# The experts' four stationary buffers moved 64 bytes off the 512-byte grid, in an encoder kernel on one Trainium2 core

## The chip, the cores and the metric

The kernel runs on one core of one Trainium2 chip. The metric is the device time of one execution in microseconds (us). Before the change it is 1674.84 us, the median of 3 runs (1674.06 to 1678.73).

## What is computed

Two sequences (`x_prompt` and `x_sample`, 512 tokens of 1024 channels each) go through one encoder layer with shared weights: RMSNorm, neighbourhood attention with 16 heads, a residual, RMSNorm, an expert-choice mixture of 16 SwiGLU experts, a residual and a last RMSNorm. All arrays are float32. The part that the change touches is the mixture of experts. Each expert takes the 64 tokens of each sequence that it scores highest:

```
aff = jax.nn.softmax(jnp.einsum('nd,de->ne', xf, router_w).astype(jnp.float32), axis=-1)
gate, idx = lax.top_k(aff.T, cap)
xs = xf[idx]
hid = jax.nn.silu(jnp.einsum('ecd,edf->ecf', xs, w_gate)) * jnp.einsum('ecd,edf->ecf', xs, w_up)
out = jnp.einsum('ecf,efd->ecd', hid, w_down) * gate[..., None].astype(xs.dtype)
y = jnp.zeros_like(xf).at[idx.reshape(-1)].add(out.reshape(-1, D).astype(xf.dtype))
```

Here `cap` is 64, the experts' width is 2048, and both sequences together give each expert 128 rows.

## The kernel before

The kernel is written by hand, engine by engine: SyncE issues the loads of weights, GpSimd gathers and scatters rows, ScalarE, VectorE and TensorE compute, and semaphores order them. Nothing is scheduled by a tool; each engine runs its instructions in the order of the code.

**Products.** A float32 product is made of three matmuls of type float32r. Every operand is split into a high part (a cast to float32r) and a rest (the value minus its high part). `products` (L1118) issues for each pair of operands high x high, high x rest and rest x high into the same PSUM bank. All its matmuls stand on line L1123. In a trace row `ps<-w_high,xt_high 128*128 128x512` the first name is the moving operand (its 512 columns stream through the array), the second the stationary one (128 x 128 values that are loaded into the array first). The load of the stationary operand is an instruction of its own in the trace, LDWEIGHTS, on a row of the engine named PEld.

**Ahead of the experts.** For each of the two sequences the normed input stands transposed in `ut_high` and `ut_rest`. Four groups of four heads follow: `project_t` makes queries and keys (the weights are stationary, 512 columns of `ut` move), `project_v` makes the values (blocks of `ut` are stationary, 256 columns of the weights move), `score`, `turn_probabilities`, `values` and `project_out` do the rest. In `values` (L1228) the stationary operand is a slice of `v` or `v_off` of one head, 64 columns or 256 bytes. The router follows, with the choice of the tokens on VectorE.

**The experts.** A loop over the 16 experts runs on every engine. The 128 gathered rows (`xg`) are transposed on TensorE (`rows_t`, L1379), ScalarE writes their high part into `xt_high` (`rows_high`, L693) and VectorE the rest into `xt_rest` (`rows_rest`, L1053). `gate_up` makes one half of the hidden width at a time: 8 pairs of weight tiles, 96 matmuls, stationary `xt_high` and `xt_rest`. The product of both branches, `hid`, is transposed (`hidden_t`, L1409) and split into `ht_high` (L697) and `ht_rest` (L1057). `down` multiplies by the other weights: 4 pairs, 48 matmuls, stationary `ht_high` and `ht_rest`. So an expert has 2 x 96 + 2 x 48 = 288 matmuls, each with 512 moving columns. Every tile of weights (1 MB, 128 x 2048 values) is loaded into `raw`, `raw_more` or `early`, cast by ScalarE into one of four slots of `w_high` (L713) and split by VectorE into `w_rest` (L779). In the last expert the second `down` takes `xt_high` and `xt_rest` as its stationary buffers (written on L756 and L1085).

**Where the buffers lie.** `sb` takes a buffer where the one before it ends. `sb_line` rounds its start up to a multiple of `LINE` = 512 bytes (in each of the 128 partitions). All large buffers are made by `sb_line`, so a moving block of 512 columns (2048 bytes) and a stationary one of 128 columns (512 bytes) both begin on this grid. In the program as built `xt_high` starts at byte 22016 (43 x 512), `xt_rest`, `ht_high` and `ht_rest` behind it, 4096 bytes each, and `raw_more` at 38400. `w_high` starts at 87552 and `w_rest` at 120320. `ut_high` starts at 22016 as well; it and the experts' buffers share the space, one after the other in time. `ident`, the moving operand of the transposes, starts at 16512, 128 bytes past a grid line.

Of the kernel before, what the change touches and what calls it, by code (L numbers as in the profile page):

```python
# [18 lines left out]
F32R = mybir.dt.float32r  # L19
# [5 lines left out]
P = 128  # L25
D = 1024
# [28 lines left out]
HALF = F // 2  # L55
BANK = 512
LINE = 512
FRONT_Q = TRUNKS * GROUPS
GU_PAIRS = 8
D_PAIRS = 4  # L60
# [50 lines left out]
def encoder_kernel(nc, x, g_mix, g_ffn_col, g_ffn, g_fin, w_qkv, bias, w_o, router_w, w_gate, w_up, w_down, identity, y):  # L111
# [5 lines left out]
    with ExitStack() as ctx:  # L117
        def sb(name, shape, dt=F32):
            return ctx.enter_context(nc.sbuf_tensor(name, shape, dt))
# [30 lines left out]
        def sb_line(name, shape, dt=F32):  # L150
            return ctx.enter_context(nc.sbuf_tensor(name, shape, dt, align_bytes=LINE))

        with ExitStack() as front:
            ut_high = front.enter_context(nc.sbuf_tensor("ut_high", [P, KC * T], F32R, align_bytes=LINE))
            ut_rest = front.enter_context(nc.sbuf_tensor("ut_rest", [P, KC * T], F32R, align_bytes=LINE))
        xt_high, xt_rest = sb_line("xt_high", [P, D], F32R), sb_line("xt_rest", [P, D], F32R)
        ht_high, ht_rest = sb_line("ht_high", [P, D], F32R), sb_line("ht_rest", [P, D], F32R)
        raw_more = sb_line("raw_more", [P, 2, PAIR])
        raw = sb_line("raw", [P, SLOTS, PAIR])
        w_high = sb_line("w_high", [P, SLOTS, PAIR], F32R)  # L160
# [6 lines left out]
        with ExitStack() as attention:  # L167
            v_off = attention.enter_context(nc.sbuf_tensor("v_off", [P, TILES - 1, GC], F32, align_bytes=LINE))
            bias_sb = attention.enter_context(nc.sbuf_tensor("bias_sb", [P, 2, 3, WIN], F32, align_bytes=LINE))
            ot_high = attention.enter_context(nc.sbuf_tensor("ot_high", [P, 2, T], F32R, align_bytes=LINE))  # L170
            ot_rest = attention.enter_context(nc.sbuf_tensor("ot_rest", [P, 2, T], F32R, align_bytes=LINE))
# [102 lines left out]
        def body_q(e, i):  # L274

            return FRONT_Q + GU_PAIRS // SLOTS + (2 * (GU_PAIRS + D_PAIRS) // SLOTS) * e + i // SLOTS

        def body_turn(e, i):

            return GU_PAIRS // RAW_SLOTS + (2 * (GU_PAIRS + D_PAIRS) // RAW_SLOTS) * e + i // RAW_SLOTS  # L280

        def pairs_before(e):

            return SLOTS * (body_q(e, 0) - FRONT_Q)

# [22 lines left out]
        def _(sp):  # L308

            def load(q, j, src):  # L310
                if not (isinstance(q, int) and q == 0):

                    sp.wait_ge(rest_done, SLOTS * (q - 1) + j + 1)
                sp.dma_start(raw[:, j, :].rearrange("p (k n) -> p k n", k=src.shape[1]), src).then_inc(raw_in[j], 16)  # L314

            def gate_up_rows(e, h, jj):
                rows_ = (w_gate, w_up)[jj % 2][bass.ds(e * D + (jj // 2) * 2 * P, 2 * P), h * HALF:(h + 1) * HALF]
                return rows_.rearrange("(k p) n -> p k n", p=P)
# [11 lines left out]
            def load_first(i):  # L330

                if i < SLOTS:
                    return load(FRONT_Q, i, gate_up_rows(0, 0, i))
                if i < SLOTS + 2:
# [176 lines left out]
        def _(act):  # L511
# [193 lines left out]
            def highs(e, lo, hi):  # L705

                for i in range(lo, hi):
                    q, before = (FRONT_Q + i // SLOTS, 0) if e is None else (body_q(e, i), body_turn(e, i))

                    act.wait_ge(pair_used, SLOTS * (q - FRONT_Q - 1) + i % SLOTS + 1)  # L710

                    act.wait_ge(raw_in[i % RAW_SLOTS], 16 * ((FRONT_Q if i % RAW_SLOTS < SLOTS else 0) + before + 1))
                    nc.scalar.copy(w_high[:, i % SLOTS, :], raws[i % RAW_SLOTS]).then_inc(high_done, 1)  # L713
# [765 lines left out]
```

## Time and profile before

| | before |
|---|---|
| median of 3 runs | 1674.84 us (1674.06 to 1678.73) |
| the profiled execution | 1675.15 us |
| its span, first to last instruction | 1673.3 us |
| mean granted TensorE clock | 0.979 |
| TensorE busy | 1590.2 us (95%) |
| VectorE busy | 1279.0 us (76%) |
| ScalarE busy | 1052.2 us (63%) |
| first matmul of the experts | 553.67 us into the span |

The profiled execution lies 1.85 us above its span; that part is outside the first and the last instruction. Busy time is the time in which an engine had at least one instruction under way; matmuls overlap each other, so the duration of one is longer than the distance to the next. The granted clock is given as a share of 2.4 GHz.

### The profile page before, as it was taken

To read this page: it belongs to the slowest core of one execution; us is meant where nothing else is said; L and a number is where in the kernel's file an instruction comes from. 1 tells how busy PE (TensorE), PEld (TensorE's weight loads), DVE (VectorE), ACT (ScalarE), POOL (GpSimd) and SP (SyncE) were. 2 spreads that over 40 slices of the span, in tenths; PEclk is the share of its full clock that TensorE was granted. 3 is DMA by queue.
4 is the path that set the end of the run, shared out by engine and by line. 5 is a ranking of instruction groups with operands and counts; after the bars stand their busy time and mean duration, and the time that the engine had idled before them with its cause. 6 is when DMAs were issued, how large, how long until landed. Compare 5 with 4: busy or idle time off the path is not lost.

```text
span 1673.3 us, 22439 instructions
## 1 busy us (share of the span) xinstructions
PE 1590.2 (95%) x8198; PEld 1322.8 (79%) x8198; DVE 1279.0 (76%) x1259; ACT 1052.2 (63%) x940; POOL 119.1 (7%) x65
## 2 busy tenths in 40 slices
PE   5999999999994799999999999999999999999993
PEld 4888787888783688888888888888888888888882
DVE  5554575554566588888888888888888888888886
ACT  4443355443343477777777777777777777777774
POOL 0000002000002001011010110100101101011011
PEclk9999999999996899999999999999999999999997
DMA  9333243533253699999999999999999999999993
GB/s 355 123 104 112 79 155 144 199 105 107 85 186 139 223 342 367 393 398 376 392 380 387 397 370 386 390 384 397 365 392 397 376 393 380 387 392 375 392 393 142
DMA packets 150326, 496.14 MB, mean 296 GB/s; under 512 B 9488, under 2 KB 34192, under 8 KB 150288
## 3 DMA queue, kind: packets, MB, share of 16 engines
q1 hardware_dynamic: 138848, 454.20, 71.8%
q0 software_dynamic: 10160, 38.28, 7.0%
q10 hardware_dynamic: 1280, 3.15, 0.7%
q8 instruction: 25, 0.41, 0.1%
q14 instruction: 13, 0.11, 0.0%
HBM read 471.47 MB, written 20.97 MB: 294 GB/s over the span
## 4 chain that ended last, share of the span: by engine, by line
PE 89%; DVE 4%; DMA 2%; ACT 2%; SPq 1%; issue 1%; ACTq 0%; DVEq 0%; POOL 0%; POOLq 0%
PE ps L1123 80%; PE ps L1197 2%; PE ps L1228 2%; PE ps L1409 2%; PE ps L1206 2%; PE ps L1328 1%; PE ps L1379 1%; DMA arena<-h_rows 1%; DVE w_rest L779 1%; DMA h_rows<-xh,rows 1%; SPq L314 1%; PE ps L1317 1%; DVE arena L812 0%; DMA rw<-router_w 0%; SPq L380 0%
## 5 line engine op out<-in xcount | busy, mean ns | idle before, releaser
L779 DVE TENSOR_TENSOR w_rest<-raw,w_high 128x2048 fp32r<-128x2048 f32 x224 | 510.3, 2290 | 98.4 <-ACT w_high L713 65.3
L713 ACT CAST w_high<-raw 128x2048 fp32r<-128x2048 f32 x188 | 360.2, 1916 | 138.2 <-PE ps L1123 138.2
L1123 PE MATMUL ps<-w_high,xt_high 128*128 128x512 f32 x1040 | 324.4, 393 | 3.9 <-DVE xt_rest L1053 2.4
L1123 PE MATMUL ps<-w_rest,xt_high 128*128 128x512 f32 x1040 | 321.2, 390 | 0.0
L1123 PE MATMUL ps<-w_high,xt_rest 128*128 128x512 f32 x1040 | 320.9, 390 | 0.0
L779 DVE TENSOR_TENSOR w_rest<-raw_more,w_high 128x2048 fp32r<-128x2048 f32 x96 | 218.6, 2290 | 48.6 <-ACT w_high L713 48.6
L779 DVE TENSOR_TENSOR w_rest<-early,w_high 128x2048 fp32r<-128x2048 f32 x96 | 218.5, 2289 | 23.0 <-ACT w_high L713 21.5
L1123 PEld LDWEIGHTS ps<-w_rest,xt_high 128*128 128x128 f32 x1040 | 195.8, 188 | 41.1
L1123 PEld LDWEIGHTS ps<-w_high,xt_rest 128*128 128x128 f32 x1040 | 195.8, 188 | 41.0
L1123 PEld LDWEIGHTS ps<-w_high,xt_high 128*128 128x128 f32 x1040 | 193.2, 188 | 43.3 <-DVE xt_rest L1053 2.8
L713 ACT CAST w_high<-raw_more 128x2048 fp32r<-128x2048 f32 x96 | 183.9, 1916 | 69.0 <-PE ps L1123 69.0
L713 ACT CAST w_high<-early 128x2048 fp32r<-128x2048 f32 x96 | 183.9, 1916 | 61.4 <-PE ps L1123 61.4
L1123 PE MATMUL ps<-w_high,ht_high 128*128 128x512 f32 x496 | 154.2, 392 | 0.0
L1123 PE MATMUL ps<-w_high,ht_rest 128*128 128x512 f32 x496 | 152.8, 389 | 0.0
L1123 PE MATMUL ps<-w_rest,ht_high 128*128 128x512 f32 x496 | 152.8, 389 | 0.0
L528 ACT ACTIVATE arena<-arena,nmx 128x256 f32<-128x256 f32 x128 | 63.6, 498 | 89.7 <-DVE nmx L827 89.7
L1123 PEld LDWEIGHTS ps<-w_rest,ht_high 128*128 128x128 f32 x496 | 93.1, 188 | 19.5
L1123 PEld LDWEIGHTS ps<-w_high,ht_rest 128*128 128x128 f32 x496 | 93.1, 188 | 19.4
L487 POOL DMA_INDIRECT h_rows<-xh,rows x15 | 37.5, 2502 | 973.2 <-ACT xh L703 973.2
L1123 PE MATMUL ps<-ut_high,w_high 128*128 128x512 f32 x256 | 103.2, 403 | 3.4 <-DVE w_rest L779 3.4
L1123 PEld LDWEIGHTS ps<-w_high,ht_high 128*128 128x128 f32 x496 | 91.9, 188 | 18.1
L1123 PE MATMUL ps<-ut_rest,w_high 128*128 128x512 f32 x256 | 100.4, 392 | 0.0
(152 smaller groups left out, 1937.9 us busy)
## 6 DMA issues: line engine op xcount, KB each, us to landing
raw<-w_gate SPq DMA_DIRECT2D x64, 1024.0 KB, 7.4
raw<-w_up SPq DMA_DIRECT2D x64, 1024.0 KB, 8.1
raw<-w_down SPq DMA_DIRECT2D x64, 1024.0 KB, 7.4
raw_more<-w_gate SPq DMA_DIRECT2D x32, 1024.0 KB, 7.9
raw_more<-w_up SPq DMA_DIRECT2D x32, 1024.0 KB, 8.8
early<-w_gate SPq DMA_DIRECT2D x32, 1024.0 KB, 8.4
early<-w_up SPq DMA_DIRECT2D x32, 1024.0 KB, 8.5
raw_more<-w_down SPq DMA_DIRECT2D x32, 1024.0 KB, 7.6
```

The source lines that it names most:

```text
L314: sp.dma_start(raw[:, j, :].rearrange("p (k n) -> p k n", k=src.shape[1]), src).then_inc(raw_in[j], 16)
L487: pool.indirect_dma_start(h_dram, bass.IndirectOffsetOnAxis(ap=rows[:, e:e + 1], axis=0), ys, None, compute_op=ALU.add).then_inc(scattered ...
L528: nc.scalar.activation(scores[hh % 2][:, i, :], scores[hh % 2][:, i, :], ACT.Exp, bias=nmx[:, hh % 2, i:i + 1], accum_out=psum_row[:, hh % ...
L713: nc.scalar.copy(w_high[:, i % SLOTS, :], raws[i % RAW_SLOTS]).then_inc(high_done, 1)
L779: nc.vector.tensor_tensor(w_rest[:, j, :], raws[j if r is None else r], w_high[:, j, :].bitcast(F32), ALU.subtract).then_inc(rest_done, 1)
L1123: done = nc.tensor.matmul(out, lhs, rhs, start=start and part == 0, stop=stop and part == 2)
L1197: last = nc.tensor.matmul(ps[:, 6 * BANK + at:6 * BANK + at + WIN], qt[on, p, tile * P:(tile + 1) * P], kt[on, p, lo:lo + WIN], start=True ...
L1206: last = nc.tensor.transpose(ps[:, at:at + P], scores[hh % 2][:, i, c * P:(c + 1) * P], ident[:, :])
L1228: last = nc.tensor.matmul(bank(4)[a * HD:(a + 1) * HD, tile * P:(tile + 1) * P], vals, pt[:, at:at + P], start=c == 0, stop=c == 1)
L1317: last = nc.tensor.transpose(bank(ROUTER_BANKS[i % 2], 2)[:, kc * P:(kc + 1) * P], xh[:, i, kc * P:(kc + 1) * P], ident[:, :])
L1328: last = nc.tensor.matmul(bank(4)[:, i * E:(i + 1) * E], rt[i % 2][:, kc * P:(kc + 1) * P], rw[:, kc, :], start=kc == 0, stop=kc == KC - 1)
L1409: last = nc.tensor.transpose(bank(6, 2)[:, c * P:(c + 1) * P], hid[:, c * P:(c + 1) * P], ident[:, :])
```

## The change

The four buffers `xt_high`, `xt_rest`, `ht_high` and `ht_rest` are no longer made by `sb_line` but by a new helper that rounds a start up to 64 bytes only, behind a buffer `shift` of 64 bytes that nothing reads or writes. In the program as built each of the four starts 64 bytes lower than before: `xt_high` at 21952, which is 448 bytes past a grid line or 64 bytes short of the next. `shift` lies at 21888. Every other buffer keeps its address, and on every engine the instructions, their order and their waits are the same. A stationary block of 512 bytes, which began on a grid line and ended on the next, now begins 64 bytes ahead of a line and crosses it.

```diff
@@ -55,6 +55,7 @@
 HALF = F // 2
 BANK = 512
 LINE = 512
+SHIFT = 64
 FRONT_Q = TRUNKS * GROUPS
 GU_PAIRS = 8
 D_PAIRS = 4
@@ -153,8 +154,11 @@
         with ExitStack() as front:
             ut_high = front.enter_context(nc.sbuf_tensor("ut_high", [P, KC * T], F32R, align_bytes=LINE))
             ut_rest = front.enter_context(nc.sbuf_tensor("ut_rest", [P, KC * T], F32R, align_bytes=LINE))
-        xt_high, xt_rest = sb_line("xt_high", [P, D], F32R), sb_line("xt_rest", [P, D], F32R)
-        ht_high, ht_rest = sb_line("ht_high", [P, D], F32R), sb_line("ht_rest", [P, D], F32R)
+        def sb_shift(name):
+            return ctx.enter_context(nc.sbuf_tensor(name, [P, D], F32R, align_bytes=SHIFT))
+
+        sb("shift", [P, SHIFT // 4])
+        xt_high, xt_rest, ht_high, ht_rest = (sb_shift(n) for n in ("xt_high", "xt_rest", "ht_high", "ht_rest"))
         raw_more = sb_line("raw_more", [P, 2, PAIR])
```

## Rows read from the trace of the kernel before

**Rows 1.** The page: busy us of each engine, share, instructions.
```profile
PE 1590.2 (95%) x8198; PEld 1322.8 (79%) x8198; DVE 1279.0 (76%) x1259; ACT 1052.2 (63%) x940; POOL 119.1 (7%) x65
```

**Rows 2.** The page: the chain that ended last, by engine and by line.
```profile
PE 89%; DVE 4%; DMA 2%; ACT 2%; SPq 1%; issue 1%; ACTq 0%; DVEq 0%; POOL 0%; POOLq 0%
PE ps L1123 80%; PE ps L1197 2%; PE ps L1228 2%; PE ps L1409 2%; PE ps L1206 2%; PE ps L1328 1%; PE ps L1379 1%; DMA arena<-h_rows 1%; DVE w_rest L779 1%; DMA h_rows<-xh,rows 1%; SPq L314 1%; PE ps L1317 1%; DVE arena L812 0%; DMA rw<-router_w 0%; SPq L380 0%
```

**Rows 3.** The chain in order of time, one expert: start us, us, what.
```profile
671.80 0.87 PE ps L1379 x8
672.67 10.90 PE ps L1123 x48
683.57 0.87 PE ps L1409 x8
684.45 32.66 PE ps L1123 x144
717.11 0.87 PE ps L1409 x8
717.98 21.78 PE ps L1123 x96
739.76 0.87 PE ps L1379 x8
```

**Rows 4.** Busy time by stretch, two experts: PE, PEld, DVE, ACT, POOL, clock, DMA.
```profile
672.67:740.63 67.96, 67.96 (x314) 56.54 (x313) 59.95 (x30) 51.36 (x31) 5.28 (x2) 1.00 1.02 391
740.63:808.59 67.96, 67.96 (x314) 56.54 (x313) 59.95 (x30) 51.39 (x31) 5.27 (x2) 1.00 1.01 380
```

**Rows 5.** Groups of TensorE by line: busy us, mean ns, idle before, releasers.
```profile
L1123 PE MATMUL ps<-w_high,xt_high 128*128 128x512 f32 x1040 | 324.4, 393 | 3.9 <-DVE xt_rest L1053 2.4 <-DVE xt_rest L1085 1.0 <-DVE w_rest L779 0.6
...
L1123 PE MATMUL ps<-w_high,ht_high 128*128 128x512 f32 x496 | 154.2, 392 | 0.0
```

**Rows 6.** Timeline of TensorE in `project_v`: start us, us, instruction.
```profile
349.07 0.28 PE L1123 MATMUL ps<-w_high,ut_rest 128*128 128x256 f32 x1
...
350.51 0.28 PE L1123 MATMUL ps<-w_high,ut_rest 128*128 128x256 f32 x1
```

**Rows 7.** Line L1228, the loads: duration ns least/median/most, first and last start us.
```profile
L1228 PEld LDWEIGHTS ps<-arena,v x256: 132/137/137, 69.4 to 495.6; 128*64 128x64 f32 x128
...
L1228 PEld LDWEIGHTS ps<-arena,v_off x256: 132/137/137, 69.7 to 495.2; 128*64 128x64 f32 x128
```

**Rows 8.** Instructions on the tiles `xt_high` and `ht_high`, same columns.
```profile
L1123 PEld LDWEIGHTS ps<-w_high,xt_high x1040: 186/188/333, 553.7 to 1646.8; 128*128 128x128 f32 x174
...
L693 ACT CAST xt_high<-ps x16: 999/1007/1012, 551.3 to 1558.0; 128x1024 fp32r<-128x1024 f32 x16
L1053 DVE TENSOR_TENSOR xt_rest<-ps,xt_high x16: 1214/1216/1224, 552.4 to 1560.6; 128x1024 fp32r<-128x1024 f32 x16
...
L697 ACT CAST ht_high<-ps x31: 999/1011/1012, 589.4 to 1608.8; 128x1024 fp32r<-128x1024 f32 x31
L1057 DVE TENSOR_TENSOR ht_rest<-ps,ht_high x31: 1216/1218/1220, 591.7 to 1611.1; 128x1024 fp32r<-128x1024 f32 x31
```

**Rows 9.** The chain in order of time, where the experts begin.
```profile
552.39 1.24 DVE xt_rest L1053
553.67 21.66 PE ps L1123 x84
```

**Rows 10.** The page: GB/s that the DMA engines moved, 40 equal slices.
```profile
GB/s 355 123 104 112 79 155 144 199 105 107 85 186 139 223 342 367 393 398 376 392 380 387 397 370 386 390 384 397 365 392 397 376 393 380 387 392 375 392 393 142
```

**Rows 11.** The chain in order of time: two pieces of the output projections.
```profile
426.20 5.67 PE ps L1123 x24
...
492.18 2.78 PE ps L1123 x12
```

## The prediction

> **What bounds the kernel now.** I read four views, from coarse to fine. The page's busy times come first: TensorE is busy for 95% of the span, VectorE for 76%, ScalarE for 63% [rows 1]. A busy share does not say who sets the end, so the chain of work that ended last comes next: 89% of it is TensorE, and 80% of the span is one line, L1123, the matmuls of `products` [rows 2]. The third view is the same chain in order of time, through one expert [rows 3]. The reader should see that nothing but TensorE stands in it: 48 + 144 + 96 = 288 matmuls in 10.90 + 32.66 + 21.78 = 65.34 us, three times eight transposes of 0.87 us, and again from the start. The fourth view, busy time by stretch, says the same of whole experts: of 67.96 us TensorE is busy for 67.96, VectorE for 59.95, ScalarE for about 51.4, at a granted clock of 1.00, which is the 2.4 GHz level [rows 4]. So in the experts the pace is set by TensorE's own distance from one matmul to the next, 65.34 us / 288 = 226.9 ns. No wait stands there for another engine to shorten or lengthen.
>
> **How many matmuls the change can reach.** The four moved buffers are the stationary operand of 3 x 1040 matmuls (`xt_high`, `xt_rest`) and 3 x 496 (`ht_high`, `ht_rest`), 4608 in all [rows 5]. Their cost now is 4608 x 226.9 ns = 1045.6 us, 62% of the span. One nanosecond per matmul is thus 4.6 us, and what a measurement of this kernel can tell from no change, about 0.3% or 5.0 us, is 1.1 ns per matmul. This is the number to watch: a very small effect of the address would show.
>
> **What the 226.9 ns are made of.** The matmuls of `project_v` have 256 moving columns in place of 512. In the timeline 12 of them follow each other from 349.07 to 350.51 us, 120.0 ns apart [rows 6]. The difference of 106.9 ns for 256 columns is 2.4 columns per ns. So 512 columns stream for 213.8 ns, by the plain 2.4 GHz for 213.3, and each matmul carries a part of about 13.3 ns that does not grow with the columns. (By 2 x 120.0 - 226.9 it is 13.1, by 226.9 - 213.3 it is 13.6; the starts are given to 0.01 us.) That fixed part is the only thing in the experts' pace that an address of the stationary operand could take away. It is the same size here, with stationary blocks of `ut_high` and `ut_rest`, and in the experts. Both of these pairs start on the 512-byte grid, so this alone cannot say whether the grid causes it.
>
> **The load of the stationary operand.** It runs beside the matmul before it. Where nothing longer covers it, its pace is seen: the eight transposes L1379 or L1409 have 128 moving columns only (53 ns at the rate above) and still take 0.87 us / 8 = 108.9 ns each [rows 3]. That is the load's own pace for 128 columns. Beside 512 moving columns it has 226.9 - 108.9 = 118 ns of cover. Each shifted block of 512 bytes starts 64 bytes below a grid line, so it touches two lines of the grid where it touched one. As an estimate take a cost of one more 64-byte piece on eight: 108.9 / 8 = 13.6 ns, hidden in the 118. With the cover gone it would be 4608 x 13.6 ns = 63 us; it would take a load more than twice as long for the cover to go. I cost it at nothing.
>
> Does an offset lengthen a load at all? The trace has a natural trial. In `values` (L1228) the stationary operand is a head's 64 columns, 256 bytes, so that every other head begins 256 bytes off the 512-byte grid. The 256 loads from `v` last 132 to 137 ns with a median of 137, and those from `v_off` the same [rows 7]. Half of each are off the grid, and no second duration appears. Such a block does not cross a grid line, so it excludes a cost of the start, not of the crossing. The transposes give the other half of the trial, for a moving operand off the grid: `ident` starts 128 bytes past a grid line and the pace is still only 2 ns above the 107 ns that 128 columns would take at half the streaming rate [rows 3].
>
> **Do the two reads meet?** The stationary block of 512 bytes is read while 2048 bytes of moving columns are read. By the paces above, one goes at about 512 / 107 = 4.8 bytes per ns and the other at 9.6. With different speeds, two readers that start on the same place of a repeating grid part at once and meet again elsewhere; a start moved by 64 bytes shifts the meetings by some 13 ns and does not remove them. That is a second reason to expect nothing, even if a collision costs something.
>
> The Trainium skill, in "SBUF — State Buffer", section "Who interferes with whom", gives TensorE two independent read ports, one for the moving operand and one for the load, and says that it never waits on another reader. By that rule the stationary operand's place changes nothing and the sum is 1675. No run here has yet shown both of its halves; the constant pace beside a busy DMA and VectorE [rows 3, 4] agrees with it.
>
> **The writes into the buffers.** ScalarE writes `xt_high` in 1.01 us and VectorE `xt_rest` in 1.22 us, 17 times each (16 of them in the row), and `ht_high` and `ht_rest` 31 times each in 1.01 and 1.22 us [rows 8]. If all became an eighth longer, VectorE would gain 48 x 0.152 = 7.3 us of work and ScalarE 6.1 us. Inside an expert that is hidden: VectorE has 67.96 - 59.95 = 8.0 us free in each of them [rows 4]. It is exposed only at the first expert and at the last one's second half, where TensorE waits for `xt_rest`, 2.4 and 1.0 us [rows 5]: 2 x (0.126 + 0.152) = 0.6 us. I take zero, with 0.6 as the upper end.
>
> **Everything else.** The change adds no instruction, no semaphore wait and no DMA, and the order on every engine is the same. `ut_high`, `ut_rest`, `raw_more` and all behind them keep their addresses, since the 64 bytes of `shift` and the move both lie in what was padding. The stages ahead of the experts' matmuls, up to 553.67 us [rows 9], should not change.
>
> **The sum.** Matmuls 4608 x 0, loads 0 (covered), writes 0 (0 to 0.6): 1675.15 us for the profiled execution, which stands 0.3 us above the median of the runs, 1674.84. I forecast 1674.8.
>
> **Rivals.**
>
> No relation or meetings that only move, so no change. For it: two different read speeds, the load with 118 ns of cover, a pace that holds through an expert to 0.1 ns while VectorE, ScalarE and DMA vary. Against it: nothing here pairs an off-grid stationary block with a stream long enough to be the bound. Time 1671 to 1679. **Chance 0.64.**
>
> Faster: the fixed 13.3 ns are the price of both reads starting on the same place of the grid, and the shift removes it. For it: in every group where it can be read, both operands are on the grid. Against it: it is equally large beside 512 and 256 moving columns. Removed whole it would be 4608 x 13.3 = 61 us, or 1614; but then an expert takes 64.1 us, and the weights must come in that time. An expert moves (391 + 380) / 2 GB/s x 67.96 us = 26.2 MB now [rows 4], and the fastest slice of the span shows 398 GB/s [rows 10], at which 26.2 MB take 65.8 us. So DMA becomes the bound after 2.1 us per expert, 16 x 2.1 = 34 us: 1641. A removal in part gives anything between. **Chance 0.15.**
>
> The Trainium skill, "TensorE: Matmul & The Clock Gate", section "Wait — 56ns, not 53.3ns?", gives a warm matmul of 512 columns a start-to-start of 215.7 ns. By that figure 11.2 of the 226.9 ns here are surplus, an estimate of 52 us for the experts. The row here stands above the page, and the page does not say what the surplus is.
>
> Slower: what now runs without a meeting begins to have one. The two reads start within a few ns of each other, on the same grid, and may be in step by luck; shifted, each load crosses a line in its first 64 bytes while the stream begins. The place is each of the 4608 starts. The price has no row of its own. The nearest is the same form of matmul where it runs slower for another reason: 12 in 2.78 us, 231.7 ns, or 24 in 5.67 us, 236.3 ns, both in output projections [rows 11]. That is +4.8 to +9.4 ns, 22 to 43 us: 1697 to 1718. I take the first, nearer to no cost. It decides from 1.1 ns on. For it: the same absence of an off-grid row. Against it: the loads of L1228 show no second duration. **Chance 0.21.**
>
> **The numbers.** The predicted time is that of the likeliest case, 1674.8, whose own range is 1671 to 1679. To leave out no more than 2 in 10 I reach to the near end of the slower rival, 1698, and down to 1668, a gain of 1.5 ns per matmul; the gain of tens of microseconds is left out. Faster by over 0.3% 0.15, within 0.3% 0.64, slower by over 0.3% 0.21.
>
> **What would show it.** Right: in the changed kernel an expert still has 10.90, 32.66 and 21.78 us in the chain, loads from `xt_high` have a median of 188 ns [rows 8], and the start of the experts stays at about 554 us. Wrong in the cover of the load: loads over 188 ns and a pace above 226.9. Wrong in the meeting of reads: the pace changes with loads unchanged. If only the writes matter, L1053 and L1057 differ from 1.22 us and the pace does not. The prediction fails if the pace moves by more than 1.1 ns per matmul either way. A change only in the first 554 us would mean that something other than the buffers' place acts.

## The result and the profile after

The changed kernel takes 1686.03 us (median of 4 runs, 1684.25 to 1688.71), the kernel before 1675.12 us beside it. The ratio is 1.0057 with a 95% interval of 1.0043 to 1.0071: slower, by about 9 to 11 us. On the page of the changed kernel one busy time grew by more than 2 us: TensorE is at 1600.1 us where it was 1590.2 [rows 1]. Its loads (PEld) are at 1324.2 for 1322.8; VectorE and ScalarE moved by 0.1 and 0.6 us.

```profile
PE 1600.1 (95%) x8198; PEld 1324.2 (79%) x8198; DVE 1278.9 (76%) x1259; ACT 1052.8 (63%) x940; POOL 119.2 (7%) x65
```

The chain in order of time through one expert shows where (start us, us, what). All lines are four higher than before, so L1127 is `products`.

```profile
672.82 0.87 PE ps L1383 x8
673.69 10.99 PE ps L1127 x48
684.68 0.88 PE ps L1413 x8
685.55 32.96 PE ps L1127 x144
718.51 0.87 PE ps L1413 x8
719.38 21.97 PE ps L1127 x96
741.36 0.87 PE ps L1383 x8
```

These answer to [rows 3]. The transposes take what they took, 0.87 us. The 288 matmuls take 10.99 + 32.96 + 21.97 = 65.92 us where they took 65.34: 228.9 ns each for 226.9. The same stands in the busy time by stretch, two experts:

```profile
673.69:742.23 68.54, 68.54 (x314) 56.58 (x313) 59.95 (x30) 51.40 (x31) 5.27 (x2) 1.00 1.01 385
742.23:810.77 68.54, 68.54 (x313) 56.58 (x313) 59.95 (x30) 51.41 (x31) 5.28 (x2) 1.00 1.01 380
```

An expert takes 68.54 us for 67.96 [rows 4], with VectorE, ScalarE and the granted clock as they were. 16 x 0.58 = 9.3 us accounts for the growth of the span, 1682.4 us for 1673.3. The chain where the experts begin is no later than before:

```profile
551.41 1.24 DVE xt_rest L1057
552.69 21.33 PE ps L1127 x84
```

And the instructions on the tile `xt_high` (duration ns least/median/most) show what did not change, against [rows 8]:

```profile
L1127 PEld LDWEIGHTS ps<-w_high,xt_high x1040: 186/188/338, 552.7 to 1655.9; 128*128 128x128 f32 x174
...
L697 ACT CAST xt_high<-ps x16: 1001/1005/1012, 550.4 to 1566.6; 128x1024 fp32r<-128x1024 f32 x16
L1057 DVE TENSOR_TENSOR xt_rest<-ps,xt_high x16: 1214/1215/1224, 551.4 to 1569.2; 128x1024 fp32r<-128x1024 f32 x16
```

The load still lasts 188 ns, the writes 1.01 and 1.22 us. So it is neither a longer load that came out of its cover nor the writes: the distance from one matmul to the next grew by 2.0 ns while everything on either side of it kept its size. That is the sign that the prediction had named for a failure in the meeting of the reads: the pace changes with the loads unchanged.

The 2.0 ns are a mean. The trace keeps each start to 1 ns, finer than the views print. In the experts of the kernel before (from 600 to 1600 us, leaving out the first dozen matmuls behind each group of transposes) every start is 226 or 227 ns after the one before it. In the changed kernel three distances take turns, 232, 226 and 229 ns on average, with high and rest blocks alike. So the price is not the same at every matmul; every third one pays none.

### The profile page after: what moved, and what is told of

It reads as the page before. It is cut to its first block, busy times and chain, and to the rows that moved or that the text cites. A ratio compares the mean times of both kernels' runs of the same rounds, so it can differ in the third digit from the quotient of the medians.

```text
span 1682.4 us, 22439 instructions
## 1 busy us (share of the span) xinstructions
PE 1600.1 (95%) x8198; PEld 1324.2 (79%) x8198; DVE 1278.9 (76%) x1259; ACT 1052.8 (63%) x940; POOL 119.2 (7%) x65
## 4 chain that ended last, share of the span: by engine, by line
PE 90%; DVE 4%; DMA 2%; ACT 1%; SPq 1%; issue 1%; ACTq 0%; DVEq 0%; POOL 0%; POOLq 0%
PE ps L1127 80%; PE ps L1201 2%; PE ps L1232 2%; PE ps L1210 2%; PE ps L1413 2%; PE ps L1332 1%; PE ps L1383 1%; DMA arena<-h_rows 1%; DMA h_rows<-xh,rows 1%; SPq L318 1%; DVE w_rest L783 1%; PE ps L1321 0%; DVE arena L816 0%; DMA rw<-router_w 0%; SPq L384 0%
## 5 line engine op out<-in xcount | busy, mean ns | idle before, releaser
L1127 PE MATMUL ps<-w_high,xt_high 128*128 128x512 f32 x1040 | 326.9, 396 | 3.8 <-DVE xt_rest L1057 2.4
L1127 PE MATMUL ps<-w_rest,xt_high 128*128 128x512 f32 x1040 | 324.9, 394 | 0.0
L1127 PE MATMUL ps<-w_high,xt_rest 128*128 128x512 f32 x1040 | 322.2, 391 | 0.0
L1127 PEld LDWEIGHTS ps<-w_high,xt_rest 128*128 128x128 f32 x1040 | 195.8, 188 | 44.7
L1127 PEld LDWEIGHTS ps<-w_rest,xt_high 128*128 128x128 f32 x1040 | 196.3, 189 | 42.7
L1127 PEld LDWEIGHTS ps<-w_high,xt_high 128*128 128x128 f32 x1040 | 193.8, 189 | 43.9 <-DVE xt_rest L1057 2.8
L1127 PE MATMUL ps<-w_high,ht_high 128*128 128x512 f32 x496 | 155.0, 394 | 0.0
L1127 PE MATMUL ps<-w_rest,ht_high 128*128 128x512 f32 x496 | 154.5, 393 | 0.0
L1127 PE MATMUL ps<-w_high,ht_rest 128*128 128x512 f32 x496 | 153.3, 390 | 0.0
L1127 PEld LDWEIGHTS ps<-w_high,ht_rest 128*128 128x128 f32 x496 | 93.1, 188 | 21.3
L1127 PEld LDWEIGHTS ps<-w_rest,ht_high 128*128 128x128 f32 x496 | 93.2, 188 | 20.1
L1127 PEld LDWEIGHTS ps<-w_high,ht_high 128*128 128x128 f32 x496 | 92.0, 188 | 18.4
L1127 PE MATMUL ps<-ut_high,w_high 128*128 128x512 f32 x256 | 103.0, 402 | 2.8 <-DVE w_rest L783 2.8
L1127 PE MATMUL ps<-ut_high,w_rest 128*128 128x512 f32 x256 | 100.5, 393 | 0.0
```

Source lines behind the costliest of these rows:

```text
L1127: done = nc.tensor.matmul(out, lhs, rhs, start=start and part == 0, stop=stop and part == 2)
```

## The experiments

Two theories were put against each other first. **R, relative**: the price hangs on the distance in bytes between the start of the stationary block and that of the moving one; in the trace the load of one runs beside the matmul that streams the other. **C, crossing**: a load that crosses a grid line costs, wherever the moving block lies. "Distance" below is the start of the stationary block less that of the moving one; all blocks start a multiple of 512 bytes from the start of their buffer. In every kernel the instructions and their order are those of before. Where a shifted buffer ends past the line on which the next one began, all buffers behind it that `sb_line` makes start one whole line of 512 bytes later, which leaves their distances as they were in steps of 256. "Pace" is the length of a piece of the chain over its count of matmuls.

**1. Everything 64 bytes below the grid.** The padding is put ahead of `ut_high`, and the alignment lowered to 64 bytes. So the distance is 0 again in `products`, while each of its loads and moving blocks crosses a line.

```diff
-LINE = 512
+LINE = 64
...
+        sb("shift", [P, 16])
+
         def sb_line(name, shape, dt=F32):
```

> All line-aligned buffers, the moving ones too, lie 64 bytes below the 512-byte grid; the distance between a stationary and a moving block is that of the kernel before. Theory R (relative: the price hangs on the distance between the start of the loaded block and that of the moving one): an expert back at 67.96 us, 226.9 ns per matmul, about 1675 us. Theory C (crossing: each load of a block that crosses a grid line costs, wherever the moving one lies): the experts stay at 228.9 ns per matmul, and the projections ahead of them get slower too, about 1686 to 1690 us.

Measured: 1678.98 us beside 1676.64, ratio 1.0009 (95% interval 0.9998 to 1.0019), which is no difference. The chain gives the experts' pace of before to the last digit:

```profile
689.04 32.66 PE ps L1125 x144
722.57 21.78 PE ps L1125 x96
745.23 10.90 PE ps L1125 x48
```

Theory C is out: the loads cross the grid's lines and cost nothing.

**2. The moving buffers 64 bytes past the grid, the stationary ones on it.**

```diff
-        w_high = sb_line("w_high", [P, SLOTS, PAIR], F32R)
-        w_rest = sb_line("w_rest", [P, SLOTS, PAIR], F32R)
+        sb("shift", [P, 16])
+        w_high, w_rest = (ctx.enter_context(nc.sbuf_tensor(n, [P, SLOTS, PAIR], F32R, align_bytes=64))
+                          for n in ("w_high", "w_rest"))
```

> The stationary buffers are on the grid as before, but w_high and w_rest start 64 bytes past it; in the experts the relative distance is that of the changed kernel. Theory R: 228.9 ns per matmul in the experts, about 1686 us, and the projections, where either the stationary or the moving block is w_high or w_rest, slower too. Theory C: loads in the experts do not cross, so 226.9 ns and about 1675 us, unless a moving block that crosses costs as well.

Measured: 1688.19 us beside 1676.64, ratio 1.0067 (1.005 to 1.0084). The experts' pieces of the chain are those of the changed kernel within 0.02 us, although no stationary buffer was moved:

```profile
689.43 32.97 PE ps L1124 x144
...
723.27 21.99 PE ps L1124 x96
...
746.14 10.99 PE ps L1124 x48
```

So R holds: what counts is the distance, here again -64 bytes. This kernel says two things more. In `project_t` the roles are turned (`w_high` is stationary, `ut_high` moves, distance +64), and there the price is larger. Two pieces of 24 matmuls in the chain, the first behind `score` (L1198, which is L1197 in the kernel before), the second behind the eight transposes on L1207 (L1206 before):

```profile
326.07 5.79 PE ps L1124 x24
...
333.91 5.61 PE ps L1124 x24
```

The same two kinds of piece in the same stretch of the kernel before:

```profile
323.49 5.67 PE ps L1123 x24
...
331.20 5.47 PE ps L1123 x24
```

Like against like, 24 matmuls take 0.12 and 0.14 us more, 5.0 and 5.8 ns each; a piece this short holds the first few matmuls too, which come at uneven distances in either kernel. In `project_v` (distance -64, 256 moving columns) the matmuls came *closer* together. The timeline, the first and the last row of a run of them:

```profile
350.13 0.28 PE L1124 MATMUL ps<-w_rest,ut_high 128*128 128x256 f32 x1
...
354.84 0.28 PE L1124 MATMUL ps<-w_high,ut_rest 128*128 128x256 f32 x1
```

The second start is 40 matmuls after the first, 4.71 us / 40 = 117.8 ns, where [rows 6] gave 120.0. With all buffers 64 bytes lower (experiment 1) the pieces of 48 of `project_v` take 5.94 and 5.95 us as before, so this too goes by the distance. The fixed 13.3 ns of the prediction are not a constant of the engine.

**3 and 4. Other distances: 128 and 256 bytes.** In the first the four buffers start at byte 21888 (no padding, alignment 64), in the second 256 bytes past a line.

```diff
-        xt_high, xt_rest = sb_line("xt_high", [P, D], F32R), sb_line("xt_rest", [P, D], F32R)
-        ht_high, ht_rest = sb_line("ht_high", [P, D], F32R), sb_line("ht_rest", [P, D], F32R)
+        sb("shift", [P, 384 // 4])
+        xt_high, xt_rest, ht_high, ht_rest = (ctx.enter_context(nc.sbuf_tensor(n, [P, D], F32R, align_bytes=32))
+                                              for n in ("xt_high", "xt_rest", "ht_high", "ht_rest"))
```

> The four stationary buffers 128 bytes below the grid in place of 64. Theory C: a crossing is a crossing, 228.9 ns per matmul, 1686 us. Theory R: a price that varies with the distance, another pace than 228.9 ns; with a grain of 128 bytes it is 226.9 ns and 1675 us.

> The four stationary buffers 256 bytes off the grid, half a line. Theory C: 228.9 ns per matmul, 1686 us. Theory R with a grain of 128 or 256 bytes: 226.9 ns and 1675 us; with a price that grows with the distance: slower than the changed kernel, over 1686 us.

Measured: 128 bytes 1701.94 us, ratio 1.0144 (1.0127 to 1.0161); 256 bytes 1676.67 us, ratio 1.0 (0.9989 to 1.001). The chain has, for the first and then for the second:

```profile
687.57 33.46 PE ps L1123 x144
```

```profile
685.98 32.66 PE ps L1124 x144
```

That is 232.4 ns per matmul at 128 bytes and 226.8 at 256. At half a line of the grid nothing is lost, though the loads cross a 512-byte line as well. A price that goes on growing with the distance is out, and so is a grain of 128 bytes; what is left is R with a repeat of 256 bytes.

**5 to 7. 32 bytes on either side, and 64 on the other side.** Same edit with paddings of 96, 160 and 192 bytes.

> The four stationary buffers 32 bytes below the grid, half the distance of the change. Theory L (the price grows with the distance up to 128 bytes: 0, 2.1, 5.5 ns at 0, 64, 128): about 227.5 to 228 ns per matmul, 1679 to 1681 us. [...]

> The four stationary buffers 32 bytes past a grid line. Theory L, symmetric: as 32 bytes below. Theory A (the sign matters, as the q and k projections of the kernel with the moved w_high suggest, 64 bytes past at 231 to 236 ns): another pace than 32 bytes below, 228 to 231 ns, 1681 to 1695 us.

> The four stationary buffers 64 bytes past a grid line in place of 64 below. Theory L, symmetric in the distance: 228.9 ns, 1686 us. Theory A: 233 ns per matmul, as the projections with 64 bytes past show, so 28 us more than before, about 1705 us. A start on any other 64-byte place being one and the same cost (crossing) is already out by the run at 256 bytes.

Measured: 32 bytes below 1707.51 us and 32 past 1707.48 us (one run each, beside 1676.32), 64 past 1703.94 us, ratio 1.0163 (1.0146 to 1.0181). The 144 matmuls of the chain:

```profile
692.14 33.59 PE ps L1124 x144
```

```profile
691.77 33.60 PE ps L1124 x144
```

```profile
690.37 33.59 PE ps L1124 x144
```

All three are 233.3 ns. The first theory L, a price that grows with the distance, fell here: 32 bytes cost three times what 64 below do. A price in steps of 64 bytes is out as well, since 32 below has neither the pace of 0 nor that of 64 below. Theory A held for 64 past (233 ns expected and measured), but its number for 32 past, 228 to 231 ns, was too low, and its claim that 32 past differs from 32 below was wrong.

**8. One part of the change alone: only `xt_high` and `xt_rest` moved.**

```diff
-        xt_high, xt_rest = sb_line("xt_high", [P, D], F32R), sb_line("xt_rest", [P, D], F32R)
+        sb("shift", [P, 16])
+        xt_high, xt_rest = (ctx.enter_context(nc.sbuf_tensor(n, [P, D], F32R, align_bytes=64)) for n in ("xt_high", "xt_rest"))
         ht_high, ht_rest = sb_line("ht_high", [P, D], F32R), sb_line("ht_rest", [P, D], F32R)
```

> One part of the change alone: xt_high and xt_rest 64 bytes below the grid, ht_high and ht_rest on it. Per-load theory: gate_up and the last down at 228.9 ns (an expert's 96 and 96 matmuls at 21.97 us each), the 96 of down at 226.9 (10.90 us for 48); 3120 of 4608 matmuls, so two thirds of the loss, about 1681.5 us. If instead the writes into the buffers or something else is behind it, the share is another.

Measured: 1684.48 us beside 1676.32, ratio 1.0051 (1.0034 to 1.0068). The chain:

```profile
721.25 21.99 PE ps L1124 x96
...
744.11 10.94 PE ps L1124 x48
```

`gate_up`, all of whose blocks are out of place, has 229.1 ns. `down`, all of whose blocks are in place, takes 10.94 us where 48 took 10.90, which looks like a pace of 227.9 ns between the two. The timeline of that piece says otherwise (a row `x2` stands for two matmuls):

```profile
744.42 0.63 PE L1124 MATMUL ps<-w_rest,ht_high 128*128 128x512 f32 x2
...
746.72 0.62 PE L1124 MATMUL ps<-w_high,ht_high 128*128 128x512 f32 x2
...
754.43 0.62 PE L1124 MATMUL ps<-w_high,ht_rest 128*128 128x512 f32 x2
```

The ten matmuls from the first to the second of these rows are 230 ns apart, the 34 from there on 7.71 us / 34 = 226.8 ns. So `down` pays nothing once it has settled; the loss sits in its first dozen matmuls. By the starts in the trace it is 0.036 us where `down` follows the transposes and 0.021 us where it follows `gate_up` directly. The price goes by which blocks are in place, as expected, with a small cost of starting on top: of the loss per expert, 0.42 us lie in the two `gate_up` and 0.06 us in the two `down`. The expected 1681.5 us lies just below the interval, which begins at 1682.0 us; 16 x 0.06 = 0.9 us of starting was not in it.

**9 to 11. 192 bytes past, 96 on either side.** Same edit with paddings of 320, 32 and 224 bytes.

> The four stationary buffers 192 bytes past a grid line. Theory P (the price repeats every 256 bytes of distance): 192 past is the same as 64 below, so 228.9 ns per matmul and 1686 us, although it is three times as far from the line. Theory D (the price rises with the distance from the line, whichever side): over 232.5 ns, about 1702 us or more.

> The four stationary buffers 96 bytes below the grid. Theory H (a start off the 64-byte pieces costs the full 6.4 ns, as at 32 bytes on either side): 233.3 ns, 1707 us. Theory B (between 64 and 128 below): 229 to 232.5 ns, 1686 to 1702 us.

> The four stationary buffers 96 bytes past a grid line. Theory H: 233.3 ns, 1707 us. A place faster than the grid, under 226.9 ns, would be seen here or at 96 below if there is one.

Measured: 192 past 1685.46 us, ratio 1.0057 (1.004 to 1.0074); 96 below 1708.4 us and 96 past 1707.21 us, one run each. For 192 past the chain is that of the changed kernel:

```profile
687.36 32.96 PE ps L1124 x144
```

Theory P held: three times as far from the line on the other side gives the same 228.9 ns, since 192 = 256 - 64. So the price repeats every 256 bytes in the two pairs tried (0 and 256, -64 and 192), and 192 past also has the turns of 232, 226 and 229 ns. Theory D, a price that rises with the distance from the line, is out. At 96 below and 96 past the same pieces are 33.61 and 33.73 us, 233.4 and 234.2 ns, which theory H (233.3 ns) expected for the first and nearly met for the second; theory B, at most 232.5, is out. Neither is faster than the grid.

**12. Only the rest buffers 64 bytes past.** `xt_high` and `ht_high` are placed on the grid first, `xt_rest` and `ht_rest` behind them, so two of each six matmuls have a stationary block out of place.

```diff
-        xt_high, xt_rest = sb_line("xt_high", [P, D], F32R), sb_line("xt_rest", [P, D], F32R)
-        ht_high, ht_rest = sb_line("ht_high", [P, D], F32R), sb_line("ht_rest", [P, D], F32R)
+        xt_high, ht_high = sb_line("xt_high", [P, D], F32R), sb_line("ht_high", [P, D], F32R)
+        sb("shift", [P, 16])
+        xt_rest, ht_rest = (ctx.enter_context(nc.sbuf_tensor(n, [P, D], F32R, align_bytes=64)) for n in ("xt_rest", "ht_rest"))
```

> Only xt_rest and ht_rest 64 bytes past a grid line (where all four gave 233.3 ns), xt_high and ht_high on it: of each six matmuls two load a block that is out of place. Price per load out of place: 2 of 6 times 6.4 ns, a mean of 229.0 ns per matmul, 1686 us, and the long distances stand at the two matmuls beside which these loads run. Price per change of place or only when all are out: another mean, 226.9 or over 231 ns.

Measured: 1697.26 us beside 1676.59, ratio 1.0116 (1.0097 to 1.0135), and in the chain:

```profile
691.16 33.28 PE ps L1124 x144
```

231.1 ns per matmul, not 229.0. A third of the blocks out of place bring two thirds of the price of all of them (4.3 of 6.5 ns). The price is not a fee per load. The expectation also placed the long distances at the two matmuls beside which the displaced blocks are loaded; they are not there. By the starts in the trace, the mean distances of the six kinds of step (from one matmul of the six to the next) lie between 228.7 and 233.4 ns, and none is at 226.7. In experiment 8, where the blocks stay in place for 48 matmuls, the pace went back to that of before; here, where the place changes twice in every six, it never does. That the changes of place are what keeps it up fits both, but no run varied their number alone.

The distances together, from the 144 matmuls of the chain and the medians (one run each for -32, 32, -96 and 96). "Worked out" is 1675.1 plus 4608 times the pace less 226.8 ns.

| distance in bytes | ns per matmul | worked out us | measured us |
|---|---|---|---|
| 0 (before; all 64 below) | 226.8 | 1675 | 1675.12; 1678.98 |
| 256 | 226.8 | 1675 | 1676.67 |
| -64 (changed kernel) | 228.9 | 1685 | 1686.03 |
| 192 | 228.9 | 1685 | 1685.46 |
| -128 | 232.4 | 1701 | 1701.94 |
| -32, 32 | 233.3 | 1705 | 1707.51, 1707.48 |
| 64 | 233.3 | 1705 | 1703.94 |
| -96 | 233.4 | 1706 | 1708.4 |
| 96 | 234.2 | 1709 | 1707.21 |

## Why the prediction was wrong

**What bounds the kernel** was right, and it is why so small an effect shows: in the experts nothing but TensorE's own pace sets the time, and 2.0 ns on 4608 matmuls are 9.3 us. The count of 4608 and the start of the experts (552.69 us for 553.67) held.

**The load** held as said: 188 ns, hidden. In all fourteen traces the loads of the experts' matmuls have a median of 187 or 188 ns. **The writes** held at zero. **Nothing ahead of the experts** became slower.

**The step that failed is "do the two reads meet".** It argued that two readers of different speed drift apart, so that a shift of 64 bytes moves their meetings and removes or adds none. Experiments 1 and 2 show that the distance decides and experiments 4 and 9 that it does so with a repeat of 256 bytes; a drift that evens all distances out would have given one pace for all. The term "matmuls 4608 x 0" was really 4608 x 2.0 ns. The drift was also thought of within one matmul, while the trace shows something carried from one matmul to the next: at a distance of 0 the starts settle to an even 226.7 ns, at -64 they go round in threes.

**The trace could not carry the step, but it held a warning.** All matmuls with 512 moving columns in the kernel before have a distance of 0 in this sense. The two natural trials that were called evidence both read something else. The loads of L1228 have their duration unchanged at 256 bytes off, but 256 bytes off is a distance without a price in the experts, and the duration of a load does not move even where there is one. The transposes with `ident` off the grid are paced by their load, so a stream that lost a few ns would be hidden. An absence of rows was written down as a reason for no change, beside the sentence that nothing paired an off-grid block with a stream long enough.

What was overlooked is that 512 moving columns do not always come at 227 ns in the kernel before either. An output projection, also at a distance of 0:

```profile
360.19 0.40 PE L1123 MATMUL ps<-w_rest,ot_high 128*128 128x512 f32 x1
...
362.05 0.39 PE L1123 MATMUL ps<-w_high,ot_high 128*128 128x512 f32 x1
...
362.96 0.39 PE L1123 MATMUL ps<-w_rest,ot_high 128*128 128x512 f32 x1
```

The first eight distances have a mean of 232 ns (from 224 to 236 ns by the starts in the trace), the next four of 227.5, and behind them it is 226 or 227 each time. So matmuls of one form, all at a distance of 0, differed by up to 12 ns within one piece. The 226.9 ns are a state into which they settle and no constant, and a change could have put another in its place. The rows of [rows 11] come from pieces like this one.

**The rule of the Trainium skill**, "SBUF — State Buffer", section "Who interferes with whom", that TensorE's two read ports are independent and that it waits on nobody, was said to agree with the trace as far as other engines go. The conclusion drawn from it, that the stationary operand's place changes nothing and the sum is 1675, does not hold here: moving one of the two blocks by 64 bytes against the other costs 2.0 or 6.5 ns per matmul, by the direction. The measurement decides. Whether it is a read that waits, no run shows.

**The rival that came** was the slower one. Its mechanism, a meeting that was avoided so far by luck, fits what was found, though a meeting itself was not shown. Its place was the 4608 starts; all of them are slower on average, but not each. Its guess at the price, 4.8 ns, was 2.4 times too large for this distance, and too small for the six that cost 5.6 to 7.4 ns. Of the two rows that gave it, 24 matmuls in 5.67 us are not a pace of 236.3 ns: behind their first six the starts are 226 or 227 ns apart, and most of the surplus is the beginning of the piece. In the 12 in 2.78 us the starts are indeed 231 ns apart on average. The case of "no change" ended at 1679 and the slower one began at 1697, so 1686.03 lies between the two, at a price that neither had: from 1.1 ns on a change was to count as slower, but no size from there to 4.8 ns was given a time. It lies inside the range of 1668 to 1698 only because that reached to the slower rival; the direction was wrong.

**The faster rival** is out for the experts. Nine distances other than 0 were tried, from -128 to 256 bytes, and none gives a mean below 226.8 ns. But its premise, that the fixed 13.3 ns may be in part a price of the place, is supported by `project_v`: 120.0 ns at a distance of 0, 117.8 at -64.

**What stays open.** Why 64 bytes below costs a third of what 64 past does, why the first dozen matmuls of a piece come unevenly, and which of the two reads waits, if one does. That the load and the stream collide in the memory is an inference from the distance, not shown by itself; no run took the load away. That memory is read in pieces of 64 bytes, which the prediction's estimate for the load and theory H take as given, no run shows either. A cost that is a multiple of 2.1 to 2.2 ns fits the paces 226.8, 228.9 and 233.3, but 232.4 and 234.2 do not fit well, and no model was settled on. A kernel faster than the one before was not found, and one that uses the gain in `project_v` was not tried: it needs a distance of -64 there, which makes it +64 in `project_t`, and 768 x 2.2 ns = 1.7 us stand against 768 x 5 to 6 ns, some 4 us.

## What to carry to other kernels

Where one engine's own pace sets the time and nothing waits, look at where its operands lie against each other, and test it: a shift by 64 bytes moved this kernel by 0.6%, one by 32 bytes by 1.9% (a single run), with not one instruction changed. For float32r matmuls of 512 moving columns, keep stationary and moving blocks a multiple of 256 bytes apart; a common grid does this, and did so as well 64 bytes below the 512-byte lines. With 256 moving columns this was not the fastest place. And a piece of the chain divided by its count mixes the beginning with the steady pace; where a nanosecond matters, read the single starts. And when a trace holds no row in which the two things differ that a change makes differ, do not read its silence as "no effect": give the unknown its own size, or find a run that separates them.

## What the runs showed of the hardware

The mean distance from one matmul of 128 x 128 by 512 float32r columns to the next, with a load for each, depends on the distance between the start addresses of the stationary and the moving block, with a repeat of 256 bytes in the two pairs tried: 226.8 ns at 0 and 256, 228.9 at -64 and 192, 232.4 at -128, 233.3 at 64 and at 32 on either side, 233.4 and 234.2 at 96 below and past. The load's median duration in the trace is 187 or 188 ns at all of them, so the trace of the load does not show it. Once settled, the single distances are 226 or 227 ns at 0 and 256, and go round as 232, 226 and 229 ns in the changed kernel and at 192. With the blocks back in place the pace is back at 226.7 ns within a dozen matmuls. With 256 moving columns the order turns round: 117.8 ns at -64 and 120.0 at 0. With both blocks 64 bytes below a 512-byte line in place of on it there was no effect (ratio 1.0009).
